# A decoder trunk on one core: the last two down units by column half, and the tail behind them in pieces of 512 columns

## What is computed

```
def _moe(xn, router, w_gu, w_down):
    ...
    for e in range(N_EXPERTS):
        y = y + gates[..., e:e + 1].astype(xn.dtype) * _swiglu(xn, w_gu[e], w_down[e])
    return y
...
x = x + _moe(hn, moe_router[l // 2], moe_w_gu[l // 2], moe_w_down[l // 2])
return _rmsnorm(x, final_norm_g)
```

## Time and profile before

| | us |
|---|---|
| median of 3 runs | 1418.53 |
| lowest and highest of them | 1417.25 and 1419.8 |
| the profiled execution, its time | 1418.73 |
| its span | 1417.0 |
| PE busy in the span | 1389.7 |
| DVE busy | 1123.2 |
| ACT busy | 937.2 |

### The profile page before, as it was taken

The page is one execution under the profiler, slowest core; times in us unless marked ns, Lnnn a source line. Parts: engine busy times, 40 slices in busy tenths (PEclk is TensorE's granted clock), DMA queues, the critical chain, the costliest instruction groups (busy, mean ns, idle before and its releaser), DMA issues.

```text
span 1417.0 us, 19751 instructions
## 1 busy us (share of the span) xinstructions
PE 1389.7 (98%) x7327; PEld 1190.2 (84%) x7327; DVE 1123.2 (79%) x878; ACT 937.2 (66%) x738; POOL 55.5 (4%) x77
## 2 busy tenths in 40 slices
PE   8989999999999999999999999999999999999997
PEld 7979999979878888888788888888888888888885
DVE  7885445576657988888898888888889888888995
ACT  5853343354656777777777777777777777777773
POOL 2002000002003000000000000000000000003000
PEclk9999999999998999999999999999999999999999
DMA  9547955659343999999999999999999999999991
GB/s 311 198 147 270 354 181 192 190 164 384 136 147 113 409 408 393 381 397 365 350 402 367 357 412 376 366 371 406 375 358 402 379 354 407 381 378 369 413 394 64
DMA packets 147772, 454.26 MB, mean 321 GB/s; under 512 B 7528, under 2 KB 50640, under 8 KB 133360
## 3 DMA queue, kind: packets, MB, share of 16 engines
q1 hardware_dynamic: 139360, 423.65, 80.0%
q0 software_dynamic: 6144, 22.12, 4.1%
q10 hardware_dynamic: 2192, 7.39, 1.3%
HBM read 429.54 MB, written 23.59 MB: 320 GB/s over the span
## 4 chain that ended last, share of the span: by engine, by line
PE 92%; DVE 3%; ACT 3%; issue 1%; DMA 0%; ACTq 0%; DVEq 0%; POOLq 0%; POOL 0%
PE bank L1284 29%; PE bank L1285 29%; PE bank L1286 29%; PE bank L1681 2%; DVE w_lo L751 1%; ACT prob L602 1%; ACT w_hi L400 1%; PE bank L1355 0%; PE bank L1689 0%; DMA rows<-in_lru_lambda 0%; DVE rc L896 0%; PE bank L1541 0%; DVE act_lo L773 0%; PE bank L1633 0%; PE bank L1397 0%
## 5 line engine op out<-in xcount | busy, mean ns | idle before, releaser
L1183 DVE TENSOR_TENSOR w_lo<-raw,w_hi 128x2048 fp32r<-128x2048 f32 x249 | 566.3, 2290 | 73.8 <-ACT w_hi L676 72.4
L676 ACT ACTIVATE w_hi<-raw 128x2048 fp32r<-128x2048 f32 x249 | 475.0, 1917 | 142.2 <-PE bank L1286 132.1
L1284 PE MATMUL bank<-w_hi,act_lo 128*128 128x512 f32 (+1 forms) x752 | 291.6, 388 | 3.4 <-issue 1.4
L1286 PE MATMUL bank<-w_hi,act_hi 128*128 128x512 f32 (+1 forms) x752 | 290.0, 386 | 0.0
L1285 PE MATMUL bank<-w_lo,act_hi 128*128 128x512 f32 (+1 forms) x752 | 289.6, 385 | 0.0
L751 DVE TENSOR_TENSOR w_lo<-raw,w_hi 128x2048 fp32r<-128x2048 f32 x67 | 153.2, 2290 | 96.4 <-ACT w_hi L400 96.3
L1183 DVE TENSOR_TENSOR alt_lo<-raw,alt_hi 128x2048 fp32r<-128x2048 f32 x84 | 192.4, 2290 | 37.4 <-ACT alt_hi L676 36.6
L676 ACT ACTIVATE alt_hi<-raw 128x2048 fp32r<-128x2048 f32 x84 | 161.0, 1917 | 43.4 <-PE bank L1286 38.8
L1284 PEld LDWEIGHTS bank<-w_hi,act_lo 128*128 128x128 f32 x752 | 141.9, 189 | 32.9 <-issue 3.3
L1284 PE MATMUL bank<-act_hi,w_lo 128*128 128x256 f32 x576 | 164.8, 286 | 1.9 <-DVE act_lo L763 1.9
L1286 PEld LDWEIGHTS bank<-w_hi,act_hi 128*128 128x128 f32 x752 | 141.5, 188 | 28.4
(11 more groups left out here) (283 smaller groups left out, 1675.9 us busy)
## 6 DMA issues: line engine op xcount, KB each, us to landing
raw<-in_moe_w_gu SPq DMA_DIRECT2D x224, 1024.0 KB, 7.6
raw<-in_moe_w_down SPq DMA_DIRECT2D x112, 1024.0 KB, 7.8
raw<-in_mlp_w_gu SPq DMA_DIRECT2D x22, 1024.0 KB, 5.2
raw<-in_mlp_w_down SPq DMA_DIRECT2D x11, 1024.0 KB, 5.0
raw<-in_lru_w_in SPq DMA_DIRECT2D x8, 1024.0 KB, 12.7
tok_rows<-zeros POOLq DMA_DIRECT2D x16, 512.0 KB, 17.2
raw<-in_w_kvf SPq DMA_DIRECT2D x8, 1024.0 KB, 5.4
raw<-in_fox_w_qg SPq DMA_DIRECT2D x8, 1024.0 KB, 5.5
```

Of the source, the lines that this page charges most:

```text
L676: a.activation(moe_slot(g)[0], raw[:, u % RAW, :], ACT.Copy).then_inc(hi_done, 1)
L1183: v.tensor_tensor(lo, raw[:, u % RAW, :], hi.bitcast(f32), ALU.subtract).then_inc(lo_done, 1)
L1284: t_.matmul(dst, l_lo, r_hi, start=start, stop=False)
L1286: return t_.matmul(dst, l_hi, r_hi, start=False, stop=stop)
```

## The change

The last job's units 40 and 41 are no longer worked through unit by unit (both halves of each) but half by half: half 0 of both units, then half 1 of both. A new counter `y_half` tells that half 0 is complete. The split of `y`, the scatter and the addition follow per half. `keep_warm(6, 6)` goes; `keep_warm(1, 6)` stands between the two halves' scatters. `y_hi` and `y_lo` move from chunks 4 to 7 to chunks 0 to 3 of `act_hi` and `act_lo`, since chunks 4 and 5 hold the hidden block that half 1 still reads. The sums of squares are made over 512 columns: three on ACT, one on DVE. POOL adds the parts in separate instructions and takes the power per block. The scaling and the output are four pieces of 128 x 512 (256 KB) in place of two of 128 x 1024. A tensor `ms4` of 16 bytes per partition is allocated after `rstd3`, ahead of `slot0` and all that follows it.

```diff
+        ms4 = sb("ms4", [P, 2, NT])
...
-        y_hi = act_hi[:, 4:8, :].rearrange("p c n -> p (c n)")
-        y_lo = act_lo[:, 4:8, :].rearrange("p c n -> p (c n)")
+        y_hi = act_hi[:, 0:4, :].rearrange("p c n -> p (c n)")
+        y_lo = act_lo[:, 0:4, :].rearrange("p c n -> p (c n)")
...
             for t in range(NT):
-                sp.wait_ge(out_ready, t + 1)
-                sp.dma_start(out[0, t * P:(t + 1) * P, :], xs[:, t, :]).then_inc(stored, 16)
-            sp.wait_ge(stored, NT * 16)
+                for half in range(2):
+                    w = slice(HALF * half, HALF * half + HALF)
+                    sp.wait_ge(out_ready, 2 * t + half + 1)
+                    sp.dma_start(out[0, t * P:(t + 1) * P, w], xs[:, t, w]).then_inc(stored, 16)
+            sp.wait_ge(stored, 2 * NT * 16)
...
-            pool.wait_ge(sq_act, 2)
-            pool.wait_ge(sq_dve, 2)
-            g.tensor_scalar(msq[:, 3, :], ss[:, 3, :], 1.0 / D, EPS, ALU.mult, ALU.add).then_inc(msq_ready, 1)
-            pool.wait_ge(msq_ready, 1)
-            g.tensor_tensor(rstd[:, 3, :], msq[:, 3, :], neghalf[:], ALU.pow).then_inc(rstd_ready, 1)
+            pool.wait_ge(sq4_act, 2)
+            g.tensor_scalar(ms4[:, 0, :], ms4[:, 0, :], EPS, None, ALU.add).then_inc(ms4_ready, 1)
+            pool.wait_ge(ms4_ready, 1)
+            pool.wait_ge(sq4_act, 3)
+            g.tensor_tensor(ms4[:, 1, 0:1], ms4[:, 0, 0:1], ms4[:, 1, 0:1], ALU.add).then_inc(ms4_ready, 1)
+            pool.wait_ge(ms4_ready, 2)
+            g.tensor_tensor(rstd[:, 3, 0:1], ms4[:, 1, 0:1], neghalf[:, 0:1], ALU.pow).then_inc(rstd_ready, 1)
+            pool.wait_ge(sq4_dve, 1)
+            g.tensor_tensor(rstd[:, 3, 1:2], ms4[:, 1, 1:2], neghalf[:, 0:1], ALU.pow).then_inc(rstd_ready, 1)
...
-                    act.wait_ge(unit_used, U_MOE + JU * j + JU)
                     if final_job:
                         for half in range(2):
+                            act.wait_ge(unit_used if half else y_half, U_MOE + JU * j + JU if half else 1)
                             a.activation(y_hi[:, HALF * half:HALF * half + HALF], bank[4 + half], ACT.Copy).then_inc(yhi_done, 1)
...
-            act.wait_ge(x_final, 1)
-            squares(3)
+            for n, (t, half) in enumerate(((0, 0), (1, 0), (0, 1))):
+                w = slice(HALF * half, HALF * half + HALF)
+                act.wait_ge(x_final, n + 1)
+                a.activation(xs[:, t, w], x[:, t, w], ACT.Square, scale=1.0 / 32, accum_out=ms4[:, half, t:t + 1]).then_inc(sq4_act, 1)
...
+            last_y_lo(0)
+            add_last(0, 0)
+            last_y_lo(1)
+            add_last(1, 0)
+            add_last(0, 1)
+            add_last(1, 1)
+            dve.wait_ge(x_final, 4)
+            dve.wait_ge(ms4_ready, 1)
+            v.tensor_tensor_reduce(out=xs[:, 1, HALF:], in0=x[:, 1, HALF:], in1=x[:, 1, HALF:], scale=1.0 / D, scalar=ms4[:, 0, 1:2],
+                                   op0=ALU.mult, op1=ALU.add, accum_out=ms4[:, 1, 1:2]).then_inc(sq4_dve, 1)
+            dve.wait_ge(gfin_loaded, 16)
+            dve.wait_ge(sq4_act, 3)
+            dve.wait_ge(sq4_dve, 1)
             for t in range(NT):
-                v.scalar_tensor_tensor(out=xs[:, t, :], in0=x[:, t, :], scalar=rstd[:, 3, t:t + 1], in1=gfin_bc[:],
-                                       op0=ALU.mult, op1=ALU.mult).then_inc(out_ready, 1)
+                dve.wait_ge(rstd_ready, 2 + t)
+                for half in range(2):
+                    w = slice(HALF * half, HALF * half + HALF)
+                    v.scalar_tensor_tensor(out=xs[:, t, w], in0=x[:, t, w], scalar=rstd[:, 3, t:t + 1], in1=gfin_bc[:, w],
+                                           op0=ALU.mult, op1=ALU.mult).then_inc(out_ready, 1)
...
+            def last_units(u, n):
+
+                for half in range(2):
+                    for i in range(2):
+                        unit_ready(u + i, n)
+                        hi, lo = moe_slot(u + i - U_MOE)
+                        for k in range(2):
+                            h = slice((2 * i + k) * P, (2 * i + k + 1) * P)
+                            w = slice(k * D + half * HALF, k * D + half * HALF + HALF)
+                            last = mm3(bank[4 + half], hid3_hi[:, h], hid3_lo[:, h], hi[:, w], lo[:, w], False, i == 1 and k == 1)
+                        if half:
+                            last.then_inc(unit_used, 1)
+                    if not half:
+                        last.then_inc(y_half, 1)
...
-            keep_warm(6, 6)
             for half in range(2):
                 w = slice(HALF * half, HALF * half + HALF)
                 pe.wait_ge(ylo_done, half + 1)
...
+                if not half:
+                    keep_warm(1, 6)
```

More of the change, by code:

```diff
@@ L213, in yoco_kernel @@
         e_silu, e_h, e_T, e_hid_hi, e_hid_lo = (sem(n) for n in ("e_silu", "e_h", "e_T", "e_hid_hi", "e_hid_lo"))
-        x_final, out_ready = sem("x_final"), sem("out_ready")
+        x_final, out_ready, y_half, sq4_act, sq4_dve, ms4_ready = (sem(n) for n in ("x_final", "out_ready", "y_half", "sq4_act", "sq4_dve", "ms4_ready"))
         def cols256(w, c):
@@ L712, in expert_pair @@
                             hid_hi_pair(j, T_AT.index(k))
-                    act.wait_ge(unit_used, U_MOE + JU * j + JU)
                     if final_job:
                         for half in range(2):
+                            act.wait_ge(unit_used if half else y_half, U_MOE + JU * j + JU if half else 1)
                             a.activation(y_hi[:, HALF * half:HALF * half + HALF], bank[4 + half], ACT.Copy).then_inc(yhi_done, 1)
                     else:
+                        act.wait_ge(unit_used, U_MOE + JU * j + JU)
                         act.wait_ge(y_stored, 16 * j + 1)
@@ L1256, in _, with last_y_lo @@
             expert_pair(pair, True)
-            for half in range(2):
+            def last_y_lo(half):
                 w = slice(HALF * half, HALF * half + HALF)
@@ L1260, in _, with add_last @@
                 v.tensor_tensor(y_lo[:, w], bank[4 + half], y_hi[:, w].bitcast(f32), ALU.subtract).then_inc(ylo_done, 1)
-            for half in range(2):
-                for t in range(NT):
-                    w = slice(HALF * half, HALF * half + HALF)
[L1264 to L1273, removed]
-                v.scalar_tensor_tensor(out=xs[:, t, :], in0=x[:, t, :], scalar=rstd[:, 3, t:t + 1], in1=gfin_bc[:],
-                                       op0=ALU.mult, op1=ALU.mult).then_inc(out_ready, 1)
+            def add_last(t, half):
+                w = slice(HALF * half, HALF * half + HALF)
+                dve.wait_ge(scattered, 2 * half + t + 1)
+                v.scalar_tensor_tensor(out=x[:, t, w], in0=bank[2 * t + half], scalar=gate_l[:, t:t + 1], in1=x[:, t, w],
+                                       op0=ALU.mult, op1=ALU.add).then_inc(x_final, 1)
+            last_y_lo(0)
[11 more added lines that the diff above has]
+            dve.wait_ge(sq4_dve, 1)
+            for t in range(NT):
+                dve.wait_ge(rstd_ready, 2 + t)
+                for half in range(2):
+                    w = slice(HALF * half, HALF * half + HALF)
+                    v.scalar_tensor_tensor(out=xs[:, t, w], in0=x[:, t, w], scalar=rstd[:, 3, t:t + 1], in1=gfin_bc[:, w],
+                                           op0=ALU.mult, op1=ALU.mult).then_inc(out_ready, 1)
         @block.tensor
@@ L1718, in expert_pair @@
                                 expert_in(u, n, k - U_AT[p], p, (bank[2], bank[3]))
-                            if D_AT[p] <= k < D_AT[p] + D_UNITS[p]:
+                            if D_AT[p] <= k < D_AT[p] + D_UNITS[p] and not (final_job and p == NPAIR - 1):
                                 expert_out(u, n, k - D_AT[p], p)
+                        if final_job and k == D_AT[NPAIR - 1]:
+                            last_units(u, n)
                         if k == TOK_AFTER and not final_job:
```

## The result

| | us |
|---|---|
| kernel before, median of 20 runs | 1418.41 |
| changed kernel, median of 20 runs | 1420.49 |
| ratio, with its 95% interval | 1.0014, 1.0007 to 1.0020 |
| profiled execution of the changed kernel: span | 1419.0 |

The forecast was 1415.8 with a range up to 1417.0. The changed kernel is not faster: it is 0.14% slower, outside the range, and its interval doesn't reach down to 1. The prediction's own "within 0.2%", which had a chance of 0.53, came true by luck: it stood for a gain just too small to be seen, and not for a loss. Two executions of the kernel before (1534 and 1977 us) and one of e4 (2798 us) stood far above all others and are left out of the ratios.

What follows compares the result with a forecast made beforehand. PE's matmul stream, 92% of the chain, was taken as unchanged, leaving the 13.97 us tail. Its terms, -1.66 - 0.96 + 0.61 - 0.67 = -2.7, put the median at 1415.8, range 1414.8 to 1417.0.

Steps and rivals of the forecast that it cites:

- within 0.2%: Whole kernel: the change in time stays within the 0.2% (2.8 us) a measurement can tell from no change; chance 0.53.
- POOL's addition for block 0: Tail, behind the squares: POOL waits for DVE's squares and ends 0.05 after them, at 1408.03, where free 1407.6.
- -1.66: Tail, up to the last addition: working half by half brings its end from 1408.86 to 1407.20.
- the filler, not the data: Before the first scatter: keep_warm ends at 1405.62, y_lo's first half near 1404.4, so the filler ends the wait.
- The 0.33 for DVE's scaling held by POOL's second power: Tail, scaling: block 1's power on POOL starts 0.04 ahead of DVE's first scaling and delays it by 0.33.
- first rival: Tail: POOL and DVE hardly meet; short power doesn't hold DVE, 1415.5; addition not held either, 1415.1; chance 0.20.
- the first sentence of the argument: PE's matmul stream, in the chain at 92%: the same before and after, so only the 13.97 us tail counts.
- the 16 new bytes: Rival, PE's stream: ms4 costs tiles behind it their 64-byte alignment, weight loads slow; 1425 at 0.235 per matmul; chance 0.05.
- Nothing in the trace ties a duration to an address: Weight loads in PE's stream: argument, beside the margin of 0.188 to 0.227, against a slowdown from moved tiles.
- losing power: Rival, scaling: POOL's second power waits through both pieces of block 0, costing 0.53 instead of 0.33; 1416.0; chance 0.12.
- falling clock: Rival, scatter: without the filler, PE's gap of 0.5 drops the clock from 2.4 to 1.2 GHz; about 1416.5; chance 0.04.

Runs made afterwards that it cites:

- e4: Changed kernel with the filler tensor at 16 elements in place of 8, tiles behind it at a multiple of 128 bytes: 1414.95 us, ratio 0.9974.
- e10: Kernel before with its two hidden tiles alone moved by 64 bytes and keep_warm(2, 6) in place of keep_warm(6, 6): 1412.55 us in one run.
- e5: Kernel before with 64 bytes allocated ahead of its first tile, so that all tiles move together: 1418.2 us, ratio 0.9998.
- e12: Kernel before with w_hi and w_lo alone moved by 32 bytes: 1436.95 us, ratio 1.0135.
- e2: Kernel before with the filler tensor at 16 elements in place of 8, moving everything behind it by 32 bytes: 1424.4 us, ratio 1.0042.
- e8: Changed kernel with its two hidden tiles alone brought back to a multiple of 128 bytes, 32 bytes allocated ahead and 96 behind: 1412.9 us, ratio 0.9965.
- e7: Kernel before with the filler tensor at 32 elements in place of 8: 1423.5 us in one run.
- e6: Kernel before with the filler tensor at 56 elements in place of 8: 1421.4 us in one run.
- e1: Changed kernel with the filler tensor at 32 elements in place of 8: 1420.9 us, ratio to the kernel before 1.0016.
- e3: Kernel before with the filler tensor at 24 elements in place of 8, moving everything behind it by 64 bytes: 1416.7 us, ratio 0.9995.

## Why the prediction was wrong

**The tail was right to within 0.1 up to the scaling.** Counted from the last unit's end (1403.03 before and 1408.00 after): y_lo of half 0 at -1.36 forecast and -1.37 measured; the first addition at +0.50 and +0.50; the second half's scatter at +1.90 and +1.91; the last addition done at +4.17 and +4.08; the scaling from +5.68 and +5.71. POOL's addition for block 0 took 0.59 and ended 0.05 behind DVE's squares, as taken from the first norm's rows. The forecast left out that more than half of the -1.66 needs no halves: its own reading that "the filler, not the data" ends the first scatter's wait is worth 0.9 by itself (e10).

**One term of it was mis-sized.** The 0.33 for DVE's scaling held by POOL's second power did not come. POOL started at 1413.57 and DVE at 1413.71, and the four scalings took 747 to 753 ns each, which is their undisturbed time:

```profile
L1296 DVE SCALAR_TENSOR_TENSOR xs<-x,rstd,gfin_bc x4: 747/748/753, 1413.7 to 1415.7; 128x512 f32<-128x512 f32 x4
```

At most 0.09 of it shows, as DVE's start 0.13 behind the first power, where I had 0.04. So that half of the first rival came true and not the other. By the Trainium skill, page "SBUF — State Buffer", section "Who interferes with whom", issue order decides who blocks. The addition behind the squares agrees with it: 0.59, ending 0.05 behind DVE. The power of one column that began 0.14 ahead of DVE doesn't: it held none of the scalings. With 0.33 back, the tail is 11.0 instead of 11.3.

**The step that failed is the first sentence of the argument**: that PE's stream "is the same before and after, since the change only reorders the last 24" matmuls. It was 5 longer. The case was among the rivals, "the 16 new bytes", with a chance of 0.05, and its figures were half right: tiles move by 32 bytes, 0.005 per matmul is enough to matter. What it had wrong was the mechanism and so the chance. I priced it by the duration of a weight load, 0.188 against 0.227, and saw a margin of a fifth; the loads stayed at 0.187 and the matmuls moved apart all the same. And I looked for an absolute alignment, to 64 bytes, where e5 and e12 show a relative one, between the tile that gives the weights and the tile that is streamed. The loss per matmul was 0.0040, and it fell on 1416 matmuls: I counted the 1128 with hidden weights that stream w tiles and left out the 288 that stream alt tiles.

The trace of the kernel before held a sign that I passed over. Its groups by form, for w_lo streamed with act_hi and with hid_hi as weights:

```profile
L1285 PE MATMUL bank<-w_lo,act_hi 128*128 128x512 f32 x720 | 280.6, 390 | 0.0
...
L1285 PE MATMUL bank<-w_lo,hid_hi 128*128 128x512 f32 x376 | 147.8, 393 | 0.0
```

On the page the first group stands at 385, but that mean mixes in 32 matmuls of 256 columns; at equal shape the means differ by 3 ns only, and those of line 1286 not at all (390 both). The pitch shows it better, 0.2270 against 0.2292. Two groups that should be equal and are not were the thing to ask about. "Nothing in the trace ties a duration to an address" passed over a difference that was there.

The losing power and the falling clock did not happen: four scalings without a gap, and a granted clock of 1.00 in the changed kernel's windows from 1408 to 1412, around its gap of 0.55, and in e10's around one just as long.

**What stays open.** Shown is that the place of the hidden tiles relative to the others makes the loss (e2, e5 and e8), and that moving the streamed tiles does the same to weights that were never slow (e12). A rule in the offset alone is not shown: e12's alt tiles became slower at offset 0, and its matmuls of 256 columns faster at 32.

Why the offset acts is argued, with one observation for it. The load of the next weights runs while the current matmul still streams (PEld is busy for 84% of the span beside PE's 98%), and both read the same memory. At 24 places of the expert stage a matmul with act weights is followed by the first one with hidden weights. In the changed kernel one of them is:

```profile
527.19 0.39 PE L1307 MATMUL bank<-alt_lo,act_hi 128*128 128x512 f32 x1
527.42 0.40 PE L1308 MATMUL bank<-alt_hi,act_hi 128*128 128x512 f32 x1
527.66 0.39 PE L1306 MATMUL bank<-w_hi,hid_lo 128*128 128x512 f32 x1
```

The matmul at 527.42 reads only tiles at offset 0; the one tile that is off is the next one's weights. Its step takes 0.235 at all 24 places, as in e2 and e7, and 0.232 or 0.233 in e6, where in the kernel before it takes 0.226. So at -32, +32 and 128 the delay is there when only the next load reads a tile that is off. At +64 (e1) it is not: 0.226 there, though the pitch between hidden weights is 0.2334. The Trainium skill, page "TensorE: Matmul & The Clock Gate", section "Part 2: What happens when you issue a matmul", says that loading the next weights takes no read bandwidth from the running matmul; the 0.235 at these places does not agree with that as it stands.

By the cases here the pattern repeats after 256 bytes (modulo 512, e3's hidden tiles are 256 from the w tiles and the act tiles 0, and both are fast) and not after 128 (e6). Offsets between multiples of 32 weren't tried, and why -64 costs a third of what +64 does is open. The total time follows the sum of the pitches only within 1 or 2 us: e3's interval allows no gain at all, and e4 and e8, equal in pitch and in code but for the padding, lie 2 apart with intervals that overlap.

The fastest kernel is e8, 1412.9: the changed kernel with its hidden tiles at the same offset modulo 256 as the w tiles, 5.1 (0.35%) under the kernel before as measured beside it, and 7.6 under the median of the changed one.

## What to carry to other kernels

A new tensor in the middle of an allocation moves all that follow, and here 32 bytes cost more than the whole edit won. For matmuls of 512 columns of this type, start the tiles that one matmul reads, weights and streamed operand, at the same address modulo 256 bytes, and look at the addresses after every new allocation; for other shapes measure it, since those of 256 columns here went the other way. Read the pitch of the stream by operand, not a matmul's or a load's duration: groups that should be equal and are not are a finding. And filler work placed to keep a clock up belongs in the sum like any other; here a third of it did as well, and 0.9 sooner.

## What the runs showed of the hardware that was not expected

- Matmuls of 512 columns of a 4-byte type, with hidden weights, follow each other after 0.227 us when weights and streamed tile have the same address modulo 256, after 0.229 at -64, and after 0.2325 to 0.2334 at -32, +32, +64 and 128; the weight load has a median of 0.187 to 0.188 in all of them.
- Moving all tiles together by 64 bytes changed nothing (ratio 0.9998), moving the w tiles alone by 32 cost 1.35%, although the matmuls of 256 columns got faster by it, from 0.1200 to 0.1184.
- The step to the next matmul was 0.235 in place of 0.226, at all 24 places of the changed kernel, where only the next matmul's weights lay in a tile that was 32 bytes off.
- A POOL addition of one column beside DVE's squares over 512 columns took 0.59, to 0.05 behind DVE's end; a POOL power of one column that began 0.14 ahead of DVE's scaling lengthened none of the four scalings.
